# Shared experts' weight tiles issued from ScalarE's DMA queue instead of SyncE's

## The chip, the cores and the metric

One core of a Trainium2 chip runs the whole program. The metric is device time in microseconds of one execution. A core has five engines that run their own instruction streams and meet through semaphores: TensorE (PE), VectorE (DVE), ScalarE (ACT), GpSimd (POOL) and SyncE (SP). SP, ACT and POOL can each issue DMAs. The transfers themselves run on 16 DMA engines of the core.

## The reference

Two transformer blocks one after the other, on 256 tokens of width 1024, all in float32. The first has two layers; each has a mixer of three attention kinds, a cross attention to a memory, and a feed-forward part. The feed-forward part of layer 1 is the one that the change touches, a mixture of 8 experts of which each token takes 2:

```python
for e in range(N_EXPERTS):                      # 8
    out = out + gate[:, e:e + 1] * swiglu(t, w_gu[e], w_down[e])
# swiglu: (silu(t @ w_gate) * (t @ w_up)) @ w_down, with 1024 -> 2816 -> 1024
```

The weights of the eight experts are 8 x 35 MB (some 277 MB by the tensors' shapes), and all of them are read. The second block (an attention with a state-space part, then a pooling part) follows and is untouched.

## The kernel before

**Weights.** `weights` is a buffer of 5 slots of 128 x 4096 floats (2 MB each). SP fills a slot with one DMA and adds 16 to `slot{s}_landed`. PE adds 1 to `slot{s}_used` on its last matmul from the slot, and SP waits for that before it fills the slot again.

**The expert stage.** When no expert has more than 96 tokens (it is so here), the kernel gathers the tokens of each expert and works in 2 groups (`g`) of 4 experts. Experts 0, 1 and 2 of a group own one pass each (`q` = 0, 1, 2), in which they use 96 of the 128 rows of the array; the fourth, the shared expert, uses the last 32 rows in all three passes. So a step, called a row here, needs four tiles: one shared and three own. A group has 11 rows for up (`HID_CHUNKS`, each 256 hidden columns) and 6 for down (`FEW_DOWN`, the last one with half-size tiles of 1 MB); there are 34 rows in all, row 0 to row 33.

`few_slots` (L95) gives the slots: the shared tile of row r lies in slot r % 2, so there are two of them; the own tiles of each row lie in slots 2, 3 and 4, one buffer each. Own tile q of row r+1 can thus only be issued when pass q of row r has been done. `few_tiles` (L2064) lists the tiles in the order shared, own 0, own 1, own 2 for each row, and SP issues that list in order. The list's first five were issued before the stage.

PE (`few_group`, L715) does in each row pass 0, 1 and 2. Ahead of pass 0 it waits for the shared tile and own 0, ahead of pass 1 for own 1, ahead of pass 2 for own 2. It releases own 2 with the first matmul of the following row (`slot_owed`), and the shared slot with a matmul of the last quartet of pass 2. Behind pass 0 of an up row stand six transposes of the row before.

ACT has one silu for each pass of an up row (L1893), from the PSUM bank that the pass filled; DVE multiplies it with the other half (L1446). In the down rows ACT has nothing to do. Between the groups PE gathers the next group's tokens and sums the results of the first (`few_gather(1)`, `few_sum(0)`).

Of the kernel before, what the change touches and what calls it, by code (L numbers as in the profile page):

```python
# [69 lines left out]
NSLOT = 5  # L70
# [24 lines left out]
def few_slots(row):  # L95

    return row % 2, [2 + q for q in range(PASSES)]


def few_count(row, s):  # L100

    return row // 2 + 1 if s < 2 else row + 1
# [15 lines left out]
class Line:  # L118
# [15 lines left out]
    def next(self, name, k=1):  # L134

        self.seen[name] = self.seen.get(name, 0) + k
        return self.at(name, self.seen[name])
# [32 lines left out]
def program(nc, d, out, stop=None):  # L170
    ctx = ExitStack()
    with ctx:
# [5 lines left out]
        def sems(name):  # L178
            if name not in sem_table:
                sem_table[name] = ctx.enter_context(nc.semaphore(name))  # L180
            return sem_table[name]
# [102 lines left out]
        bank_mem = [ctx.enter_context(nc.psum_tensor(f"bank{i}", [P, 512], F32)) for i in range(4)]  # L284
        pairs = Banks("pair", 2, pair_mem)
        banks = Banks("bank", 4, bank_mem)
        jobs, tiles_used = {}, [0]
        ended_in = {}

        block = ctx.enter_context(nc.Block())  # L290
# [24 lines left out]
        def _(pe):  # L315
# [493 lines left out]
            def moe():  # L809
                pe.wait_ge(*L.next("chosen_ready"))  # L810

                upper, ones = const[:, C_UPPER:C_UPPER + P], const[:, C_ONES:C_ONES + P]
                o = begin(banks, ("places",))
                mm(o[:, 0:8], upper, chosen[:, 0, :], start=True, stop=True)
                mm(o[:, 8:16], ones, chosen[:, 0, :], start=True, stop=False)
                mm(o[:, 8:16], upper, chosen[:, 1, :], start=False, stop=True)
                mm(o[:, 16:24], ones, chosen[:, 0, :], start=True, stop=False)
                end(mm(o[:, 16:24], ones, chosen[:, 1, :], start=False, stop=True))
                pe.wait_ge(*L.next("count_ready"))
                largest = pe.value_load(most_i[0:1, 0:1], min_val=0, max_val=T)  # L820
                start = (counts(), list(pairs.uses), list(banks.uses), tiles_used[0], dict(L.seen))

                def begun():
                    return {k: v - start[0][k] for k, v in counts().items()}
                pairs.next = banks.next = 0
                rounds.update({s: sum(n % NSLOT == s for n in range(tiles_used[0])) for s in range(NSLOT)})
                with pe.If(largest < FEW + 1):
                    few_gather(0)
                    few_group(0)
                    few_gather(1)  # L830
                    few_sum(0)
                    few_group(1)
                    few_sum(1)
                    assert begun() == IN_FEW, begun()

                    for i in range(2):
                        for t in range(NT):
                            pe.wait_ge(*emptied(("few_sum", 1, i, t)))
                    pe.sem_inc(sems("banks_filled"), to_come("banks_filled", IN_FEW["banks_filled"]))
                    for s in range(2):  # L840
                        more = ALL_ROUNDS - few_count(FEW_ROWS - 2 + s, s)
                        pe.sem_inc(sems(f"slot{s}_landed"), 16 * more)
                        pe.sem_inc(sems(f"slot{s}_used"), more)
                few_seen = dict(L.seen)
                filled[0] = start[0]["banks_filled"]
                pairs.uses, banks.uses, tiles_used[0], L.seen = start[1], start[2], start[3], start[4]
                with pe.Else():

                    for s in range(NSLOT):
                        pe.wait_ge(*L.at(f"slot{s}_landed", 16 * (rounds[s] + 1)))  # L850
                        pe.sem_inc(sems(f"slot{s}_used"), 1)
                    tiles_used[0] += NSLOT
                    loop_experts(N_EXPERTS, PER_EXPERT, lambda: ffn_body(("ffn", 1)))
                    assert begun() == EACH, begun()

                    for i in range(2):
                        ring, b, _, _ = jobs[("ffn", 1), "down", i]
                        pe.wait_ge(*L.at(ring.emptied(b), ring.uses[b]))
                    pe.wait_ge(*L.at(f"slot{(tiles_used[0] - 1) % NSLOT}_used", tiles_used_at(0)))
                    for s in range(NSLOT):  # L860
                        pe.sem_inc(sems(f"slot{s}_landed"), 16 * (ALL_ROUNDS - EACH_ROUNDS))
                        pe.sem_inc(sems(f"slot{s}_used"), ALL_ROUNDS - EACH_ROUNDS)
                    if to_come("banks_filled", EACH["banks_filled"]):
                        pe.sem_inc(sems("banks_filled"), to_come("banks_filled", EACH["banks_filled"]))
                filled[0] = start[0]["banks_filled"] + max(EACH["banks_filled"], IN_FEW["banks_filled"])
                for ring in (pairs, banks):
                    for i in range(ring.n):
                        name = ring.emptied(i)
                        ring.uses[i] = start[0][name] + max(EACH[name], IN_FEW[name])
                assert tiles_used[0] == start[3] + NSLOT * EACH_ROUNDS  # L870
                tiles_used[0] = start[3] + NSLOT * ALL_ROUNDS
                L.seen = few_seen
# [913 lines left out]
                odd()  # L1786


        @block.scalar
        def _(act):  # L1790
            L = Line(act, sems)
# [69 lines left out]
            for l in range(DEPTH):  # L1861
# [17 lines left out]
                if on(f"ffn{l}"):  # L1879
                    if l == 0:  # L1880
                        ffn_body(("ffn", l))
                    else:
                        act.wait_ge(*L.next("top_gap"))
                        act.activation(rstd[:, :, 1], rstd[:, :, 0], ACT.Exp).then_inc(sems("second_exp"), 1)
                        act.wait_ge(*L.next("count_ready"))
                        largest = act.value_load(most_i[0:1, 0:1], min_val=0, max_val=T)
                        with act.If(largest < FEW + 1):
                            for g in range(N_GROUPS):
                                for c in range(HID_CHUNKS):
                                    for q in range(PASSES):  # L1890
                                        act.wait_ge(*filled(("few_up", g, c, q)))
                                        o, _ = bank(("few_up", g, c, q))
                                        act.activation(few_silu[:, (PASSES * c + q) % 4, :], o[:, 0:256], ACT.Silu)\  # L1893
                                           .then_inc(sems("few_silu_done"), 1)
                        with act.Else():
                            with L.loop(N_EXPERTS, PER_EXPERT):
                                ffn_body(("ffn", l))
                    root()
# [137 lines left out]
        def _(sp):  # L2036
# [3 lines left out]
            def load(src, width):  # L2040

                i = n[0]
                n[0] += 1
                into(i % NSLOT, i // NSLOT, src, width)

            def into(s, before, src, width):
                if before:
                    sp.wait_ge(*L.at(f"slot{s}_used", before))
                sp.dma_start(weights[:, s, 0:width], src).then_inc(sems(f"slot{s}_landed"), 16)

            def stream(src, k_tiles, widths, group):
                for c, k0, nk, w, off in weight_tiles(k_tiles, widths, group):
# [7 lines left out]
                    load(down[:, k0 * 1024:(k0 + nk) * 1024], nk * 1024)  # L2060
                    k0 += nk


            def few_tiles(first):  # L2064

                rounds = [sum(i % NSLOT == s for i in range(first)) for s in range(NSLOT)]
                row = 0
                for g in range(N_GROUPS):
                    mine = [GROUP * g + SHARED] + [GROUP * g + q for q in range(PASSES)]
                    parts = [("moe_up", c * 4096, 4096) for c in range(HID_CHUNKS)]  # L2070
                    parts += [("moe_down", 1024 * sum(FEW_DOWN[:i]), 1024 * nk) for i, nk in enumerate(FEW_DOWN)]
                    for name, at, width in parts:
                        shared, owns = few_slots(row)
                        for e, s in zip(mine, [shared] + owns):
                            yield s, rounds[s] + few_count(row, s) - 1, d[name][e][:, at:at + width], width
                        row += 1

            sp.dma_start(h[:, :, :], d["x"].rearrange("(t p) n -> p t n", p=P)).then_inc(sems("x_landed"), 16)
            sp.dma_start(norm_par[:, 0, :, :].rearrange("p a n -> p (a n)"), d["norms"][0:1, :].to_broadcast([P, 2 * D]))\
# [3 lines left out]
            for l in range(DEPTH):  # L2083
# [14 lines left out]
                if on(f"ffn{l}"):  # L2098
                    if l == 0:
                        expert(d["ffn_up"][0], d["ffn_down"][0])  # L2100
                    else:
                        first = n[0]
                        order = list(few_tiles(first))
                        for tile in order[:NSLOT]:
                            into(*tile)
                        sp.wait_ge(*L.next("count_ready"))
                        largest = sp.value_load(most_i[0:1, 0:1], min_val=0, max_val=T)
                        with sp.If(largest < FEW + 1):
                            for tile in order[NSLOT:]:
                                into(*tile)  # L2110
                        n[0] = first + NSLOT
                        with sp.Else():
                            before = n[0]
# [172 lines left out]
```

## Time and profile before

| | |
|---|---|
| Median of 3 runs | 2481.23 us (2477.7 to 2481.24) |
| Profiled execution | 2480.64 us, of which the span 2478.8 us |
| PE busy | 2300.5 us, 93% of the span |
| DVE, ACT, POOL busy | 26%, 9%, 2% |
| Queue of SP's DMAs | 466.03 MB, 47.2% of the 16 engines' span |
| Expert stage | some 715 us of the span, from 1153 to 1868 us |

Busy time is the time in which an engine has an instruction running; several matmuls that run side by side in parts of the array count once. The span is from the first to the last instruction, and the execution's own time is 1.8 us longer. A DMA line gives the time from the issue to the landing of the last of its 16 parts. L numbers are lines of the kernel; L324 is the helper through which all matmuls go, L2049 the line that issues all weight tiles.

### The profile page before, as it was taken

Reading aid. Unit: us, or ns where it says so; the run is one execution under the profiler, and the core shown is the slowest. Engines: PE = TensorE matmul, PEld = TensorE weight load, DVE = VectorE, ACT = ScalarE, POOL = GpSimd, SP = SyncE. Lnnn points to the kernel's source line nnn. Section 1 sums busy time; section 2 is a strip of 40 time slices with the busy share of each in tenths; the row PEclk is TensorE's granted clock in tenths of the full one; section 3 lists DMA queues with packets and bytes.
Section 4 is the critical chain, followed back from the end, with each engine's and each line's share of the span. In section 5 each row is a group of like instructions: output and inputs, shape, how many; then the busy total and the mean of one; then the engine's idle time right before and its main releaser. Section 6 shows DMA issues by size and latency. Waiting matters only on the chain.

```text
span 2478.8 us, 25691 instructions
## 1 busy us (share of the span) xinstructions
PE 2300.5 (93%) x11554; PEld 1128.5 (46%) x11554; DVE 636.6 (26%) x1124; ACT 233.7 (9%) x493; POOL 54.7 (2%) x58
## 2 busy tenths in 40 slices
PE   7998999899899979988999999999997998787998
PEld 3444445787344434443333333333333455443683
DVE  2433312200114242233001002001004066963011
ACT  0122001000001310010000000000000024210000
POOL 0000000000000000000000000000000000320000
PEclk9999999999999999998999999999998999678999
DMA  7304432433522044133999987999986411014340
GB/s 319 134 18 153 170 140 98 170 127 111 214 111 95 26 179 169 68 159 153 388 390 392 402 358 312 387 391 390 403 358 259 157 68 52 0 44 194 119 153 17
DMA packets 38816, 486.13 MB, mean 196 GB/s; under 512 B 4352, under 2 KB 4384, under 8 KB 7472
## 3 DMA queue, kind: packets, MB, share of 16 engines
q1 hardware_dynamic: 35264, 466.03, 47.2%
q0 software_dynamic: 3440, 18.42, 2.0%
q8 instruction: 94, 1.54, 0.2%
q14 instruction: 18, 0.15, 0.0%
HBM read 483.38 MB, written 1.05 MB: 195 GB/s over the span
## 4 chain that ended last, share of the span: by engine, by line
PE 88%; DVE 10%; issue 1%; ACT 0%; DMA 0%; POOL 0%; DVEq 0%; ACTq 0%; PEldq 0%; POOLq 0%
PE pair L324 55%; PE bank L324 33%; DVE big L1620 2%; DVE att L1103 1%; DVE big L1715 1%; DVE stats L1120 1%; DVE h L1162 1%; DVE big L1728 0%; DVE hT L1103 0%; DVE big L1103 0%; DVE h L1158 0%; DVE prob L1240 0%; DVE big L1704 0%; DMA h<-in_x 0%; DVE att L1179 0%
## 5 line engine op out<-in xcount | busy, mean ns | idle before, releaser
L324 PE MATMUL pair<-weights,hT 128*128 128x512 f32 (+1 forms) x1384 | 613.8, 600 | 7.4 <-DVE hT L1103 7.4
L324 PE MATMUL bank<-weights,att 128*32 128x512 f32 x4224 | 457.8, 593 | 0.0
L324 PEld LDWEIGHTS pair<-weights,hT 128*128 128x128 f32 x1384 | 261.6, 193 | 326.9 <-issue 314.3
L324 PE MATMUL pair<-weights,big 128*32 128x512 f32 (+1 forms) x1968 | 396.0, 592 | 3.4 <-ACT big L1840 1.7
L324 PEld LDWEIGHTS bank<-weights,att 128*32 128x32 f32 x4224 | 135.0, 110 | 306.5 <-issue 306.3
L324 PEld LDWEIGHTS pair<-weights,big 128*32 128x32 f32 (+1 forms) x1968 | 153.6, 133 | 235.6 <-issue 231.0
L324 PE MATMUL pair<-hT,weights 128*128 128x256 f32 x960 | 207.6, 379 | 0.8 <-DVE hT L1103 0.8
L324 PEld LDWEIGHTS pair<-hT,weights 128*128 128x128 f32 x960 | 182.3, 190 | 26.2 <-DVE hT L1103 1.0
L1103 DVE COPY big<-pair 128x1024 f32<-128x1024 f32 (+2 forms) x53 | 58.5, 1104 | 356.8 <-PE pair L324 356.8
L1446 DVE TENSOR_TENSOR big<-head_gain,bank 128x256 f32<-128x256 f32 x66 | 27.8, 421 | 422.5 <-ACT head_gain L1893 422.5
L324 PE MATMUL pair<-weights,att 128*128 128x512 f32 x256 | 115.9, 608 | 10.5 <-DVE att L1339 6.0
L1103 DVE COPY att<-bank 64x512 f32<-64x512 f32 (+4 forms) x120 | 69.8, 603 | 206.9 <-PE bank L324 206.5
L324 PE MATMUL bank<-att 64*128 64x256 f32 (+3 forms) x288 | 84.0, 427 | 16.9 <-DVE att L1103 10.3
L1893 ACT ACTIVATE head_gain<-bank 128x256 f32<-128x256 f32 x66 | 25.4, 384 | 600.8 <-PE bank L324 600.8
L324 PEld LDWEIGHTS pair<-weights,att 128*128 128x128 f32 x256 | 49.0, 193 | 70.4 <-issue 67.6
L324 PE MATMUL bank<-weights,big 128*32 128x512 f32 x704 | 77.8, 592 | 0.0
L324 PEld LDWEIGHTS bank<-att 128*128 128x128 f32 (+2 forms) x288 | 52.4, 194 | 46.9 <-issue 18.8
L324 PE MATMUL bank<-const,big 128*128 128x128 f32 (+2 forms) x328 | 46.3, 294 | 12.2 <-DVE big L1211 9.3
L1827 ACT ACTIVATE prob<-bank,smax 128x256 f32<-128x256 f32 x64 | 29.8, 470 | 264.4 <-DVE smax L1230 264.4
L324 PE MATMUL bank<-const,h 128*128 128x128 f32 x96 | 18.2, 370 | 38.9 <-DVE h L1162 38.9
L324 PE MATMUL bank<-probT,big 128*64 128x256 f32 (+1 forms) x192 | 48.9, 387 | 3.2 <-ACT probT L1798 3.2
L324 PEld LDWEIGHTS bank<-const,big 128*128 128x128 f32 (+2 forms) x328 | 38.6, 135 | 26.7 <-DVE big L1211 11.7
(221 smaller groups left out, 1288.4 us busy)
## 6 DMA issues: line engine op xcount, KB each, us to landing
weights<-in_moe_up SPq DMA_DIRECT2D x88, 2048.0 KB, 11.0
weights<-in_moe_down SPq DMA_DIRECT2D x40, 2048.0 KB, 11.6
weights<-in_w_in SPq DMA_DIRECT2D x18, 2048.0 KB, 7.4
weights<-in_ffn_up SPq DMA_DIRECT2D x11, 2048.0 KB, 7.2
weights<-in_even_in SPq DMA_DIRECT2D x10, 2048.0 KB, 7.8
weights<-in_mem_wkv SPq DMA_DIRECT2D x8, 2048.0 KB, 7.3
weights<-in_odd_in SPq DMA_DIRECT2D x8, 2048.0 KB, 7.2
norm_par<-in_norms POOLq DMA_DIRECT2D x10, 1024.0 KB, 7.3
```

What stands on the lines that cost most here:

```text
L324: ins = pe.matmul(o, lhsT, rhs, **flags)
L1103: ve.tensor_copy(dst, src(o)).then_inc(free, 1)
L1120: ins = ve.bn_stats(stats[:, t, c, :], src[:, t, 512 * c:512 * c + 512])
L1162: ins = ve.scalar_tensor_tensor(h[:, t, :], h[:, t, :], rstd[:, t, 0:1], b, ALU.mult, ALU.add)
L1446: ve.tensor_tensor(few_hid[:, c % 2, q, :], few_silu[:, (PASSES * c + q) % 4, :], o[:, 256:512], ALU.mult).then_inc(free, 1)
L1620: link(ve.tensor_tensor(o, a, b, op))
L1715: ins = ve.tensor_tensor_scan(scanned[:, c, i, :], rho[:, j:j + 1].to_broadcast([P, T]), w[:, i, :], 0.0, ALU.mult, ALU.add)
L1827: ins = act.activation(p, src, ACT.Exp, bias=smax[:, i % 2, t:t + 1], scale=1.0 if masked else scale, accum_out=ssum[:, i % 2, t:t + 1])
L1893: act.activation(few_silu[:, (PASSES * c + q) % 4, :], o[:, 0:256], ACT.Silu)\
```

## The change

In the expert stage the shared tiles from row 2 on (32 tiles, slots 0 and 1) leave SP's list, and ACT issues them. In the up rows ACT does so ahead of the first silu of a row: in row r it issues the shared tile of row r+1. Behind the up rows of group 0 it issues six, behind those of group 1 five. Each keeps its wait for `slot{s}_used` and its landing semaphore. SP keeps the own tiles in their order. `into` and `few_tiles` move up so that both engines can use them. All other loads stay.

```diff
+        def into(eng, L, s, before, src, width):
+            if before:
+                eng.wait_ge(*L.at(f"slot{s}_used", before))
+            eng.dma_start(weights[:, s, 0:width], src).then_inc(sems(f"slot{s}_landed"), 16)
...
                         with act.If(largest < FEW + 1):
+                            shared = [tile for tile in list(few_tiles(moe_first[0]))[NSLOT:] if tile[0] < 2]
+                            ahead = iter(shared)
                             for g in range(N_GROUPS):
                                 for c in range(HID_CHUNKS):
                                     for q in range(PASSES):
+                                        if q == 0 and (g, c) != (0, 0):
+                                            into(act, L, *next(ahead))
                                         act.wait_ge(*filled(("few_up", g, c, q)))
                                         o, _ = bank(("few_up", g, c, q))
                                         act.activation(few_silu[:, (PASSES * c + q) % 4, :], o[:, 0:256], ACT.Silu)\
                                            .then_inc(sems("few_silu_done"), 1)
+                                for _ in FEW_DOWN:
+                                    tile = next(ahead, None)
+                                    if tile is not None:
+                                        into(act, L, *tile)
...
                         with sp.If(largest < FEW + 1):
                             for tile in order[NSLOT:]:
-                                into(*tile)
+                                if tile[0] >= 2:
+                                    into(sp, L, *tile)
```

## Rows read from the trace of the kernel before

**Rows 1.** The page: span, and the chain that ended last, by engine.

```profile
span 2478.8 us, 25691 instructions
...
PE 88%; DVE 10%; issue 1%; ACT 0%; DMA 0%; POOL 0%; DVEq 0%; ACTq 0%; PEldq 0%; POOLq 0%
```

**Rows 2.** Windows: the whole expert stage, and one of its up rows.

```profile
core 0: us, PE busy (x) PEld busy (x) DVE busy (x) ACT busy (x) POOL busy (x), PEclk, DMA share, GB/s
1153.00:1868.00 715.00, 714.94 (x6466) 229.67 (x6462) 62.34 (x110) 26.65 (x67) 0.00 (x0) 1.00 0.92 377
1303.80:1325.34 21.54, 21.54 (x200) 6.77 (x199) 2.13 (x5) 1.16 (x3) 0.00 (x0) 1.00 0.96 395
```

**Rows 3.** Timeline (start, duration): an up row's end; SP issues own 2.

```profile
1296.31 0.38 ACT L1893 ACTIVATE head_gain<-bank 128x256 f32<-128x256 f32 x1 [6.50 <-PE bank L324]
...
1297.06 0.33 SPq L2049 DMA_DIRECT2D weights<-in_moe_up  x1
```

**Rows 4.** SP's issues behind it: own 2; then shared, own 0, own 1.

```profile
weights<-in_moe_up SPq DMA_DIRECT2D x1, 2048.0 KB, 9.2
...
L2049 SPq DMA_DIRECT2D weights<-in_moe_up x3: 327/328/431, 1297.4 to 1310.9; - x3
...
DMA to landing us min/median/max: 10.3/12.9/13.7
```

**Rows 5.** Timeline: weight load that opens pass 2, and SP's next issue.

```profile
1353.34 0.13 PEld L324 LDWEIGHTS bank<-weights,att 128*32 128x32 f32 x4 [0.30 <-issue]
...
1354.00 0.33 SPq L2049 DMA_DIRECT2D weights<-in_moe_up  x1
```

**Rows 6.** DMA views: a tile alone; one beside q0's; packets from 1113 to 1118 us.

```profile
weights<-in_moe_up SPq DMA_DIRECT2D x1, 2048.0 KB, 7.2
...
weights<-in_moe_up SPq DMA_DIRECT2D x1, 2048.0 KB, 11.5
...
q1 hardware_dynamic: 85, 1.39, 65.1%
q0 software_dynamic: 92, 0.75, 35.5%
```

**Rows 7.** L2049, shared to own 1: first row, worst up, worst down, last.

```profile
L2049 SPq DMA_DIRECT2D weights<-in_moe_up x3: 328/328/431, 1168.2 to 1181.7; - x3
...
DMA to landing us min/median/max: 9.7/12.5/13.2
...
weights<-in_moe_up SPq DMA_DIRECT2D x1, 2048.0 KB, 14.2
...
L2049 SPq DMA_DIRECT2D weights<-in_moe_down x3: 328/328/972, 1797.9 to 1810.2; - x3
...
DMA to landing us min/median/max: 11.8/13.6/14.1
...
L2049 SPq DMA_DIRECT2D weights<-in_moe_down x3: 327/327/432, 1839.1 to 1851.7; - x3
...
DMA to landing us min/median/max: 6.5/8.9/12.2
```

**Rows 8.** Row 16: own 2 and the shared tile issued; landings; pass 2 opens.

```profile
1487.17 0.33 SPq L2049 DMA_DIRECT2D weights<-in_moe_down  x1
...
1487.55 0.43 SPq L2049 DMA_DIRECT2D weights<-in_moe_up  x1
...
weights<-in_moe_down SPq DMA_DIRECT2D x1, 1024.0 KB, 4.9
...
weights<-in_moe_up SPq DMA_DIRECT2D x1, 2048.0 KB, 10.5
...
1492.56 0.13 PEld L324 LDWEIGHTS bank<-weights,big 128*32 128x32 f32 x4 [0.30 <-issue]
```

**Rows 9.** Windows: a PE pause of 3.43 us, and the stretch behind it.

```profile
201.93:205.36 3.43, 0.00 (x1) 0.00 (x0) 3.20 (x13) 0.55 (x1) 0.00 (x0) 1.00 0.91 306
205.80:209.20 3.40, 3.27 (x16) 2.41 (x14) 2.57 (x4) 0.00 (x0) 0.00 (x0) 0.50 0.77 251
```

More of the change, by code:

```diff
@@ L286, in program @@
         banks = Banks("bank", 4, bank_mem)
-        jobs, tiles_used = {}, [0]
+        jobs, tiles_used, moe_first = {}, [0], [0]
         ended_in = {}
@@ L825, in moe @@
                 pairs.next = banks.next = 0
+                moe_first[0] = tiles_used[0]
                 rounds.update({s: sum(n % NSLOT == s for n in range(tiles_used[0])) for s in range(NSLOT)})
@@ L1786, in _, with few_tiles @@
                 odd()
+        def into(eng, L, s, before, src, width):
+            if before:
+                eng.wait_ge(*L.at(f"slot{s}_used", before))
+            eng.dma_start(weights[:, s, 0:width], src).then_inc(sems(f"slot{s}_landed"), 16)
+        def few_tiles(first):
+            rounds = [sum(i % NSLOT == s for i in range(first)) for s in range(NSLOT)]
+            row = 0
+            for g in range(N_GROUPS):
+                mine = [GROUP * g + SHARED] + [GROUP * g + q for q in range(PASSES)]
+                parts = [("moe_up", c * 4096, 4096) for c in range(HID_CHUNKS)]
+                parts += [("moe_down", 1024 * sum(FEW_DOWN[:i]), 1024 * nk) for i, nk in enumerate(FEW_DOWN)]
+                for name, at, width in parts:
+                    shared, owns = few_slots(row)
+                    for e, s in zip(mine, [shared] + owns):
+                        yield s, rounds[s] + few_count(row, s) - 1, d[name][e][:, at:at + width], width
+                    row += 1
         @block.scalar
@@ L2043, in load @@
                 n[0] += 1
[L2044 to L2049, printed above, removed]
+                into(sp, L, i % NSLOT, i // NSLOT, src, width)
             def stream(src, k_tiles, widths, group):
@@ L2061, in expert @@
                     k0 += nk
[L2064 to L2076, printed above, removed]
             sp.dma_start(h[:, :, :], d["x"].rearrange("(t p) n -> p t n", p=P)).then_inc(sems("x_landed"), 16)
@@ L2109, in _ @@
                             for tile in order[NSLOT:]:
-                                into(*tile)
+                                if tile[0] >= 2:
+                                    into(sp, L, *tile)
                         n[0] = first + NSLOT
```

## The prediction

> **What bounds the kernel now.** Read first the page's chain of waits, for which engine sets the end: PE holds 88% of it and DMA none [rows 1]. Then the stretch that the change touches, by windows: in the 715.00 us of the expert stage PE is busy 714.94 us, in one up row 21.54 of 21.54 us, at granted clock 1.00, so 2.4 GHz [rows 2]. There is no pause in which PE waits for a tile. The DMA engines are close behind: 0.92 of the stage, 0.96 of that row. So PE sets the time, and each tile lands a few us ahead of the pass that needs it. The question is which tile has how much to spare, and in what order they come. That is read from the DMA landings, one issue at a time.
>
> Take the row whose pass 2 ends at about 1296.3 us, where ACT's silu starts [rows 3]. SP issues own 2 of the next row (call it row r) at 1297.06 and the shared tile of row r+1 right behind it at 1297.43. Own 2 lands after 9.2 us, the shared tile after 13.7, own 0 after 12.9, own 1 after 10.3 [rows 4]. Own 2 is needed when pass 2 of row r opens. The weight load that opens a pass 2 stands at 1353.34, and SP's issue of own 1, which the end of pass 1 releases, at 1354.00 [rows 5]: the deadline is some 0.65 us before own 1's issue. Here that is 1310.9 - 0.65 = 1310.3, and own 2 landed at 1306.3: 4.0 us to spare. The shared tile landed at 1311.2 and has until row r+1 opens, near 1318. So today's order on SP's queue is the right one: the urgent tile first, the patient one behind it.
>
> **The change part by part.**
>
> *SP loses 32 issues.* One is 0.33 us of a queue that otherwise waits for PE [rows 3]. Own 2 still waits for the same release, and own 0, own 1 for theirs. Nothing is earlier: 0.
>
> *ACT gains 32 waits and issues.* In an up row the wait is for the end of the row before, which has passed when ACT gets there, since the silu of that row's pass 2 stands ahead of it. The next silu is 6.5 us away [rows 3], so an issue of about 0.33 us (SP's; the trace has none on ACT) is hidden. Queued behind the waiting instruction are silus alone, and DVE's product and the bank behind them; if the cover were gone, each issue would cost PE at most its own 0.33 us. In the down rows ACT has no other work. In the gathering between the groups it has none either. 0, with bounds 0 and 32 x 0.33 = 10.6 us, and I take 0.
>
> *The shared tile is issued a little earlier.* In an up row ACT can issue when its silu is over, 1296.31 + 0.38 = 1296.69, against 1297.06 for own 2: a lead of 0.37 us. In a down row there is no silu, and the lead is 1297.06 - 1296.31 = 0.75 us. PE doesn't wait for this tile, so the lead alone is worth nothing.
>
> *Own 2 and the shared tile now lie on two queues.* This is the term that counts. The nearest rows are those where POOL's queue q0 works beside SP's q1, from 1113 to 1118 us: 92 packets of the one and 85 of the other, that is packet by packet in turn, though q0's were half as large (0.75 MB to 1.39) [rows 6]. A tile issued there landed after 11.5 us, against 7.2 alone [rows 6]. In turn, two tiles of 2 MB that start together both end when both are done. So own 2 would land where the shared tile lands now, less the lead. Were the shared tile served wholly first, own 2 would end there as well; only a preference for own 2 would spare it.
>
> The Trainium skill says the same of queues in general: its page "DMA: Bandwidth & Descriptors", section "Queues, rings and completion order", has each DMA engine take turns between its queues packet by packet, and the section "Issuing engines are not separate DMA queues" says that issuing from several engines saves only the sequencers' time. It speaks against the change: by it there is no more bandwidth to be had, and the urgent tile has to share. The trace agrees as far as it has two queues at once [rows 6].
>
> *The price by rows.* Own 2's lateness in a row is (issue of the shared tile + its landing time) - (issue of own 1 - 0.65) - lead. In the example: 1297.43 + 13.7 - 1310.3 = 0.9, less 0.37 = 0.5 us. I worked it out for the 30 rows of full tiles between the first pair and the last [rows 7]; 20 are up, 10 down. The first: 1168.2 + 13.2 - 1181.0 = 0.4, less 0.37: nothing. The worst up row: landing 14.2, 1.4 late, less 0.37 = 1.0. The worst down row: 1797.95 + 14.1 - 1809.5 = 2.5, less 0.75 = 1.8 (down rows lack the transposes, so their deadline comes 0.9 us sooner). The last: 1839.1 + 12.2 - 1851.05 = 0.25, less 0.75: nothing. Over the up rows 8 of 20 are late and add up to 2.7 us; of the down rows 6 of 10, with 4.9 us. A stall doesn't breed the next: own 0 and own 1 of the following row are issued before it, on the same queue and with the same bytes ahead of them.
>
> *Row 16* is a case by itself. Its tiles are of 1 MB, its passes half as long, and beside its own 2 goes a full shared tile for row 17. Own 2 is issued at 1487.17, lands after 4.9 us at 1492.1, and pass 2 opens at 1492.56: 0.5 us to spare. The shared tile lands at 1487.55 + 10.5 = 1498.05 [rows 8]. In turn own 2 comes at 1498.05 - 0.75 = 1497.3: 4.7 us of stall. PE has nothing else there, and all behind it (the rest of row 16, the gathering) moves along. After a pause of 3.43 us at clock 1.00 the next 3.40 us ran at 0.50, 1.2 GHz [rows 9]. Such a stretch costs half of itself: 3.4 / 2 = 1.7 us more.
>
> Row 33 has the small tiles too, but no shared tile is behind its own 2: 0.
>
> *Sum.* 2.7 + 4.9 + 4.7 + 1.7 = 14.0 us. Ahead of each weight load PE's loader idles 0.30 us [rows 5], so a tile may be 0.3 us later without moving a matmul: with that, 1.3 + 3.2 + 4.4 + 1.7 = 10.6. What it costs PE to take up again after a wait no row shows; I let the two stand against each other and take the middle, 12.3. Against the profiled execution's 2480.64 us that gives 2493 us; this execution is 0.6 us below the median of the runs shown, so it serves for both. Bounds: with no lead at all the terms are 6.8 + 10.4 + 5.5 + 1.7 = 24.4 us (2505); with own 2 always in time, 0 (2481).
>
> **The rivals.**
>
> *Own 2 is in time after all: 2481.* The mechanism is a preference: two hardware queues might be served in the order in which a tile's work reached them, or ACT's start later by more than the 4.0 us that own 2 has to spare above, so that own 2 is through first. It decides in row 16: own 2 has 0.5 us to spare there, and everything hinges on whether it is ahead of the shared tile. For it: q0 beside q1 is a software queue, not a second hardware one, and the late landings hang on the slowest of the 16 parts, which may be slower in the profiled execution than in others. Against it: the turns of [rows 6]. If only the spread of the parts shrank, row 16 would stay and the time be 2481 + 6 = 2487. Chance of no change from this: 0.22.
>
> *Faster.* The shared tile's lead fills some of the DMA engines' pause at each row's start, and SP's queue is free sooner. It could only pay where PE waits for a tile, and the stage holds 0.06 us of such time [rows 2]: 2480.6 at best. Chance 0.04.
>
> *Much slower.* The packets of two hardware queues hinder each other. A row moves 8 MB in 21.54 us, with the DMA engines busy 0.96 of it [rows 2]. If the two tiles that share (9.2 of 13.7 us) took 10% more, own 2 would be 1 us later in all 32 rows, and 2493 + 28 = 2521. Against it: the 1113 to 1118 us stretch moved 2.14 MB in 5 us, 428 GB/s, no less than one queue's best. Chance 0.06, of which half beyond my range.
>
> **How the numbers follow.** The forecast, own 2 late by sharing in turn, has 0.68. Its time is 2493 and its own range 2486 to 2505. Some 5 us, 0.2%, is what a measurement here can tell from no change. Slower by more than that: forecast and the heavy case, 0.74, less 0.02 for a forecast that comes out small: 0.72. Same: 0.24. Faster: 0.04. The range takes in the case of no change at its lower end and the bound without a lead at its upper one: 2480 to 2506.
>
> **What the profile of the changed kernel would show.** Right: PE busy below the stage's length for the first time, by some 10 us, with a pause of 4 to 5 us at row 16, ahead of the matmuls of its pass 2, and a granted clock of 0.50 behind it. Own 2's landing goes from 7 to 10 us to 11 to 14 in each row, the shared tile's from 12 to 14 by little. ACT's issues start 0.4 us (up) or 0.75 us (down) before SP's. A second hardware queue with some 65 MB. The period of most up rows stays 21.54 us, that of the late ones grows by under 1.5. Wrong: own 2 landing in 7 to 10 us as now, own 0 or own 1 later than 13 us (then the model of the order is wrong), silus delayed by ACT's issues, or pauses in rows that I have as in time.

## The result: 15 us slower, and the profile after

The changed kernel takes 2494.86 us (median of 5 runs, 2491.78 to 2501.76) against 2479.5 us before. The ratio is 1.0064, 95% interval 1.0048 to 1.0081. Measured again on another chip (e5 below) it came to 2495.73 against 2479.02 us, 1.0062 (1.0049 to 1.0075). The forecast was 2493 us, with 0.72 on slower by more than 0.2%.

The page of the kernel after: queues (q1 is SyncE's, q10 ScalarE's; packets, MB, share of 16 engines' span), and the chain that ended last. Against [rows 1], DMA now has a share of the chain.

```profile
span 2493.0 us, 25691 instructions
...
q1 hardware_dynamic: 30656, 401.02, 40.5%
q10 hardware_dynamic: 4608, 65.01, 6.9%
...
PE 82%; DVE 10%; DMA 6%; issue 1%; ACT 0%; POOL 0%; DVEq 0%; ACTq 0%; PEldq 0%; POOLq 0%
...
PE pair L324 52%; PE bank L324 30%; DMA weights<-in_moe_up 4%; DMA weights<-in_moe_down 3%; DVE big L1621 2%; DVE att L1104 1%; DVE big L1716 1%; DVE stats L1121 1%; DVE h L1163 0%; DVE big L1729 0%; DVE hT L1104 0%; DVE big L1104 0%; DVE h L1159 0%; DVE prob L1241 0%; DVE big L1705 0%
```

Windows of the kernel after: the expert stage, now some 732 us long. PE was busy all of it in [rows 2]; now 11.7 us are missing. (The window is 17 us longer: the stage itself by 15.7, and it starts 0.9 later.)

```profile
core 0: us, PE busy (x) PEld busy (x) DVE busy (x) ACT busy (x) POOL busy (x), PEclk, DMA share, GB/s
1153.00:1885.00 732.00, 720.33 (x6478) 225.57 (x6470) 62.30 (x110) 26.58 (x67) 0.00 (x0) 1.00 0.91 368
```

Waits of the kernel after in the stage (us in total, times, longest). No line of this kind stood there before. The loader's waits (PEld) and the matmuls' (PE) are the same pauses seen twice.

```profile
PEld bank L324 <- DMA weights<-in_moe_up: 13.2, 9, 2.7
PEld bank L324 <- DMA weights<-in_moe_down: 12.4, 7, 3.9
PE bank L324 <- DMA weights<-in_moe_down: 6.5, 4, 3.0
PE bank L324 <- DMA weights<-in_moe_up: 5.0, 5, 1.8
```

All of these waits come in pass 2. The timeline of the kernel after at the end of row 1, against [rows 3]: ACT issues the shared tile (L1793 is the common `into`) 0.75 us ahead of SP's own 2, and then the landings of the two.

```profile
1189.54 0.38 ACT L1917 ACTIVATE head_gain<-bank 128x256 f32<-128x256 f32 x1 [6.50 <-PE bank L324]
1189.55 0.34 ACTq L1793 DMA_DIRECT2D weights<-in_moe_up  x1
...
1190.30 0.33 SPq L1793 DMA_DIRECT2D weights<-in_moe_up  x1
...
weights<-in_moe_up ACTq DMA_DIRECT2D x1, 2048.0 KB, 15.2
...
weights<-in_moe_up SPq DMA_DIRECT2D x1, 2048.0 KB, 15.1
```

The worst of the up rows was in [rows 7] a shared tile with 14.2 us, and nobody waited for it. Here own 2 itself needs 15.1.

**The rule that ties a row's length to a landing.** In the 20 up rows of full tiles, the time from one own 2's issue to the next is 21.54 us and what own 2's landing exceeds 13.55 us. Worked out from the issues and landings of the kernel after:

| Row | own 2 lands after | row lasts | 21.54 + (landing - 13.55) |
|---|---|---|---|
| 2 | 15.07 | 23.06 | 23.06 |
| 9 | 14.88 | 22.87 | 22.87 |
| 22 | 14.23 | 22.23 | 22.22 |
| 24 | 13.69 | 21.68 | 21.68 |
| 26 | 12.89 | 21.54 | (in time) |
| 27 | 15.57 | 23.56 | 23.56 |

The 13.55 is fitted to these rows; with it the rule holds in all 20 within 0.01 us, and with the same number in the second trace of this kernel and in e1, e2, e8 and e9. So in the up rows the whole loss is own 2's lateness; nothing else lengthens a row.

**Row 16.** Timeline of the kernel after at the start of its pass 2, then windows: the pause and what follows. [Rows 8] had the matmuls run through here.

```profile
1503.99 0.20 PEld L324 LDWEIGHTS bank<-weights,big 128*32 128x32 f32 x8 [3.89 <-DMA weights<-in_moe_down]
1503.99 1.94 PE L324 MATMUL bank<-weights,big 128*32 128x512 f32 x8 [2.98 <-DMA weights<-in_moe_down]
...
1501.01:1503.99 2.98, 0.00 (x0) 0.00 (x0) 1.22 (x1) 0.00 (x0) 0.00 (x0) 0.90 1.04 443
1503.99:1507.50 3.51, 3.51 (x20) 0.91 (x24) 0.14 (x1) 0.00 (x0) 0.00 (x0) 0.60 1.00 429
```

Own 2 of row 16 landed after 8.9 us instead of 4.9, PE paused 2.98 us, and the clock was at 0.60 on average in the 3.5 us behind, as after the pause of [rows 9]. (The clock of 0.90 in the pause itself says that some 0.6 us of the half-clock stretch lay in it, where it cost nothing; the rest cost 1.4 us.) From own 2 of row 16 to own 2 of row 17 it takes 14.85 us in place of 10.30, 4.5 more.

The stage's account, by differences of these row lengths against before:

| | up rows | down rows | row 16 | sum |
|---|---|---|---|---|
| predicted, strict deadline | 2.7 | 4.9 | 6.4 | 14.0 |
| predicted, deadline 0.3 later | 1.3 | 3.2 | 6.1 | 10.6 |
| changed kernel | 6.9 | 4.2 | 4.5 | 15.7 |
| the same, second trace | 4.6 | 5.6 | 4.8 | 14.9 |

The two profiled executions before and after are 14.2 us apart (2480.64, 2494.86); the program outside the stage came out 1.5 us shorter in the second. Traces of kernels that do not lose (e3, e4 below) have sums of 0.4 to 0.6, so a difference of some tenths says nothing.

### The profile page after: what moved, and what is told of

Its sections match the earlier page's. It is cut to its first block, busy times and chain, and to the rows that moved or that the text cites. A ratio compares the mean times of both kernels' runs of the same rounds, so it can differ in the third digit from the quotient of the medians.

```text
span 2493.0 us, 25691 instructions
## 1 busy us (share of the span) xinstructions
PE 2303.2 (92%) x11554; PEld 1124.1 (45%) x11554; DVE 636.0 (26%) x1124; ACT 233.6 (9%) x493; POOL 54.6 (2%) x58
## 3 DMA queue, kind: packets, MB, share of 16 engines
q10 hardware_dynamic: 4608, 65.01, 6.9%
## 4 chain that ended last, share of the span: by engine, by line
PE 82%; DVE 10%; DMA 6%; issue 1%; ACT 0%; POOL 0%; DVEq 0%; ACTq 0%; PEldq 0%; POOLq 0%
PE pair L324 52%; PE bank L324 30%; DMA weights<-in_moe_up 4%; DMA weights<-in_moe_down 3%; DVE big L1621 2%; DVE att L1104 1%; DVE big L1716 1%; DVE stats L1121 1%; DVE h L1163 0%; DVE big L1729 0%; DVE hT L1104 0%; DVE big L1104 0%; DVE h L1159 0%; DVE prob L1241 0%; DVE big L1705 0%
## 5 line engine op out<-in xcount | busy, mean ns | idle before, releaser
L324 PE MATMUL bank<-att 64*128 64x256 f32 (+3 forms) x288 | 85.9, 434 | 16.7 <-DVE att L1104 10.1
L324 PEld LDWEIGHTS bank<-weights,big 128*32 128x32 f32 x704 | 22.5, 111 | 62.1 <-issue 49.6
## 6 DMA issues: line engine op xcount, KB each, us to landing
weights<-in_moe_up SPq DMA_DIRECT2D x68, 2048.0 KB, 11.7
weights<-in_moe_down SPq DMA_DIRECT2D x30, 2048.0 KB, 11.6
```

The lines of the kernel that those rows point to most:

```text
L324: ins = pe.matmul(o, lhsT, rhs, **flags)
```

## Experiments

All times are against runs of the kernel before on the same chip. "Stage" is the sum of row differences in one trace, as in the table above (for e7 and e10 with 0.8 us of row 17).

| Run | what | median, before | ratio (95%) | stage |
|---|---|---|---|---|
| e1 | one queue, shared tile ahead of own 2 | 2487.18, 2479.98 | 1.0031 (1.0020 to 1.0042) | +9.1 |
| e2 | change, but row 17's tile on SP | 2486.9, 2479.98 | 1.0035 (1.0021 to 1.0049) | +5.2 |
| e3 | before, small DMAs on ACT | 2479.28, 2479.98 | 1.0000 (0.9991 to 1.0009) | +0.6 |
| e4 | change, half the shared tile | 2480.32, 2479.98 | 1.0001 (0.9992 to 1.0010) | +0.4 |
| e5 | the change again | 2495.73, 2479.02 | 1.0062 (1.0049 to 1.0075) | +14.9 |
| e6 | only row 17's tile on ACT | 2484.18, 2479.02 | 1.0024 (1.0015 to 1.0032) | +5.1 |
| e7 | shared tile held until own 2 lands | 2521.44, 2479.02 | 1.0157 (1.0125 to 1.0188) | +46 |
| e8 | e1 without row 16 | 2485.94, 2479.02 | 1.0033 (1.0020 to 1.0046) | +4.3 |
| e9 | change without the head start | 2489.37, 2481.27 | 1.0035 (1.0021 to 1.0048) | +9.5 |
| e10 | shared tile held until pass 0 ends | 2485.7, 2481.27 | 1.0022 (1.0012 to 1.0031) | +7.4 |
| e11 | e1 without the head start | 2490.12, 2479.51 | 1.0050 (1.0037 to 1.0064) | +8.0 |
| e12 | change, own 2 given the head start | 2480.83, 2479.51 | 1.0007 (0.9998 to 1.0016) | +1.6 |

Theory 1 is the forecast's: what costs is own 2 coming behind the shared tile's bytes. The first rival is that ScalarE's issues, or a second queue as such, cost.

**e1, the order alone.**

```diff
+rest = order[NSLOT:]
+for i in range(len(rest) - 1):
+    if rest[i][0] == 4 and rest[i + 1][0] < 2:        # own 2, then the next row's shared tile
+        rest[i], rest[i + 1] = rest[i + 1], rest[i]
```

> All weight tiles stay on SyncE's queue; in each row the shared tile of the next row is issued ahead of own 2 instead of behind it. Theory 1 (the loss comes from own 2 landing behind the shared tile's bytes, whatever queue they are on): own 2 lands 11 to 14 us after its issue, row 16 loses about 4.5 us and the late rows some 3 to 10 us more, so 8 to 15 us slower than before. Rival 2 (it is the second hardware queue, or ScalarE's issues, that cost time): within 2 us of before, for there is neither here. Rival 3 (both: the order costs, and two queues spread the landings further): slower than before by 6 to 10 us, and by less than the changed kernel.

7.2 us slower, with no second queue and nothing new on ACT. So the order by itself costs, in this run about half of the change's loss (e11 below, another one-queue version, lost 10.6). Its waits in the stage:

```profile
PEld bank L324 <- DMA weights<-in_moe_down: 11.6, 7, 3.9
PE bank L324 <- DMA weights<-in_moe_down: 5.8, 5, 3.0
PEld bank L324 <- DMA weights<-in_moe_up: 3.3, 4, 1.1
```

Row 16's pause of 3.0 us is as in the changed kernel and the down rows are near it (3.6 us, against 4.2 and 5.6); the up rows are not (0.6 us in all, against 6.9 and 4.6). That is the outcome of the third theory.

**e2 and e6, row 16.** e2 gives row 17's shared tile back to SP, e6 leaves only that one on ACT (ACT's side of the edit is not printed here).

```diff
 # e2, SP; e6 has != 16
-    if tile[0] >= 2:
+    n_shared += tile[0] < 2
+    if tile[0] >= 2 or n_shared == 16:
         into(sp, L, *tile)
```

> The changed kernel, with one of the 32 shared tiles (that of row 17, beside the half-size own 2 of row 16) back on SyncE's queue behind own 2. Theory 1: the pause of 2.98 us and the 3.4 us at half clock at row 16 go, 4.5 us faster than the changed kernel, so some 10 us slower than before. Rival 2 (ScalarE's issues or the second queue as such): one issue in 32, 0.5 us faster than the changed kernel.

> The kernel before with one of the 32 shared tiles, that of row 17, on ScalarE's queue. Both theories: own 2 of row 16 lands some 4 us later, a pause of 3 us and 3.4 us of half clock, 4.5 us slower than before; no pause anywhere else.

e6 cost 5.2 us in its median and 5.0 us at row 16 in its trace, with no other row longer by more than 0.2: one tile of 32 makes a third of the loss. The windows of e6 show it; PE is busy 335.00 of 335.00 us ahead of row 16.

```profile
1153.00:1488.00 335.00, 335.00 (x3098) 104.21 (x3094) 23.83 (x46) 12.66 (x33) 0.00 (x0) 1.00 0.93 380
1490.00:1510.00 20.00, 16.60 (x98) 6.57 (x91) 6.34 (x9) 0.00 (x0) 0.00 (x0) 0.91 1.00 427
```

e2 kept 6.9 us of the loss, where some 10 were expected; in its trace row 16 lasts as before, which is the 4.5 us, but the late rows make 5.2 where the change's two traces had 11.1 and 10.1. Why they cost less there is not shown. The two together, 1.0035 and 1.0024, come near the change's 1.0062.

**e3, ScalarE's share.** The 32 waits and issues on ACT, with 2 KB in place of the tile.

```diff
 for q in range(PASSES):
+    if q == 0 and (g, c) != (0, 0):
+        small(next(ahead))      # waits for the shared slot, DMA of 128 x 16 bytes to a spare buffer
     act.wait_ge(*filled(("few_up", g, c, q)))
```

> The kernel before, with every tile on SyncE's queue, and ScalarE in addition doing the 32 waits of the change at its places and issuing behind each a DMA of 128 x 16 bytes (2 KB, into a spare buffer) instead of the tile. Theory 1: ScalarE's waits and issues are hidden, within 2 us of before. Rival 2a (the waits and issues on ScalarE delay silus, products and banks): 5 to 15 us slower, as the changed kernel.

The same as before. ScalarE's waits and issues are hidden, and the rival that blamed them falls.

**e4, fewer bytes on the second queue.** ScalarE loads the first half of each shared tile.

```diff
-into(act, L, *tile)
+into(act, L, s, before, src[:, 0:width // 2], width // 2)
```

> The changed kernel, but ScalarE loads only the first half of each shared tile (the rest of the slot keeps old data, so part of the shared experts' sums is left out). Theory 1: the two tiles that share have 3 MB instead of 4, own 2 lands some 2.4 us sooner (9 to 12 us after its issue), under the deadline of 13.5 us in nearly all rows; row 16 still has 2 MB in place of 3 to wait for, its pause falls from 3 us to under 1; in all 0 to 3 us slower than before. Rival 2 (the second queue or ScalarE's issues as such): the number of issues is the same, 10 to 15 us slower than before.

The same as before, with as many issues on as many queues. In the up rows own 2 landed after 9.6 us on average (10.6 at most); only row 16 had a wait left:

```profile
PEld bank L324 <- DMA weights<-in_moe_down: 1.4, 1, 1.4
PE bank L324 <- DMA weights<-in_moe_down: 0.5, 1, 0.5
```

A second queue as such, with 32 half tiles on it, costs nothing. The bytes that own 2 has to share with do.

**e5, the change again; e8, e1 without row 16.**

> The changed kernel as it is, on the same chip as the next three. Swapping the order on one queue cost 7.2 us, the change as first measured 15. Theory 1 (order alone): the excess is chance or the chip, and it comes out 7 to 11 us slower than before. Theory 3 (two queues add a spread of landings to the cost of the order): 13 to 17 us slower again.

> One queue, order swapped as before, but not for row 16 (own 2 of row 16 ahead of the shared tile of row 17). Theory 1: the 4.9 us at row 16 go, 2 to 4 us slower than before is left from the late rows.

e5 shows that the change's excess over e1 is no chance; against e11 the intervals leave it open. e8 is a miss by its time: 6.9 us slower, hardly less than e1's 7.2, where 2 to 4 were expected. In its trace row 16 lasts 10.30 us again and the late rows add 4.3, as expected; its five runs lie between 2482.93 and 2489.49 and the profiled one is the lowest. So what the late rows cost differs by some us from run to run, and e8 doesn't resolve row 16; e6 does, with 11 runs.

**e7 and e10, the shared tile held back.** Both were meant to give own 2 the engines for itself.

```diff
 # e7, behind the silu of pass 0; e10 waits for "slot2_used" (the end of pass 0)
+act.wait_ge(*L.at("slot4_landed", 16 * own_2[0]))
 into(act, L, s, before, src, width)
```

> The changed kernel, but ScalarE waits for the landing of own 2 before it issues the shared tile, and does so behind the first silu of the row. 32 tiles are on the second queue as in the change. Theory 1: own 2 lands 7 to 10 us after its issue again, no pause at row 16, and the shared tile now shares with own 0 and own 1, which have time; 0 to 3 us slower than before. Rival 2 (a second queue as such costs): 8 us or more slower than before.

> The changed kernel, but ScalarE issues each shared tile only when pass 0 of the row is over (it waits for slot 2's release, as SyncE does for own 0), so level with own 0, 6 us behind own 2. Holding it back to own 2's landing made the kernel 39 us slower, for the shared tile was issued 8 to 9 us later than before and had only 7 us to spare. Theory 1 with that: own 2 lands after 7 to 10 us as before, no pause at row 16; shared tile and own 0 land 12 to 14 us after their issue, 18 to 20 into the row, where 20.9 is the deadline: 0 to 6 us slower than before. Rival 2 (a second queue as such costs): 10 us or more.

e7 failed by far, and it isn't the queue: own 2 landed after 7.2 to 9.7 us, and row 16 had no pause. Another tile became the late one. Timeline of e7 in one row, with the landing of its shared tile:

```profile
1221.99 0.33 ACTq L1793 DMA_DIRECT2D weights<-in_moe_up  x1
...
weights<-in_moe_up ACTq DMA_DIRECT2D x1, 2048.0 KB, 14.5
...
1236.50 3.49 PE L324 MATMUL bank<-weights,att 128*32 128x512 f32 x20 [2.96 <-DMA weights<-in_moe_up]
```

1221.99 + 14.5 = 1236.5: PE stands until the shared tile is there. It was issued 9.1 us behind own 2, where before it was 0.4, and had 7 us to spare; the expectation counted own 2's time and not this tile's. e10, which holds it back to 6.1 us behind own 2 (e7: 7.2 to 9.8), lost 4.4 us, inside what was expected, with waits at the rows' starts. So the shared tile has a deadline too, and of the orders tried here the one before meets both, and e12's all but once.

**e9, e11 and e12, the head start.** In e9 ScalarE also waits for the release of own 2, so that both tiles are issued in the same 0.01 us. e11 does so in e1. e12 adds two silus on a spare buffer, so that own 2 is 0.90 us ahead.

```diff
+act.wait_ge(*L.at("slot4_used", own_2[0]))
+for _ in range(2):                                  # e12 only
+    act.activation(spare[:, 256:512], spare[:, 0:256], ACT.Silu).then_inc(sems("paused"), 1)
+    act.wait_ge(*L.next("paused"))
 into(act, L, s, before, src, width)
```

> The changed kernel, but ScalarE waits in addition for the release that SyncE waits for before own 2, so that the shared tile is issued level with own 2 and not 0.75 us ahead. Own 2's end is set by the bytes of both, so it should come later by the lead. In two traces of the changed kernel a row is longer than 21.54 us by exactly what own 2's landing exceeds 13.55 us; with 0.75 us more on each landing that rule gives 14 more. Theory 1: 22 to 30 us slower than before. Rival 4 (own 2 is late only because the shared tile's packets are ahead of it when it comes, so that level is better): at most 10 us slower.

> One queue, order swapped, but SyncE waits for own 2's release ahead of the shared tile, so the two are issued 0.4 us apart at the time of today's own 2, and the head start of 0.8 us is gone. Without the head start two queues lost 8 us instead of 15: the last of the 16 parts then came 1.4 us behind the first, not 2.2. Theory 5 (a head start while own 1's last parts still land spreads the landings, whatever the queue): the spread falls from 1.8 to some 1.4 here too, own 2 lands 12 to 13.5 us after its issue; 5 to 8 us slower than before, most of it at row 16. Rival (the spread belongs to two queues): it stays at 1.8, 7 to 12 us slower.

> The changed kernel, but ScalarE waits for own 2's release and then runs two silus on a spare buffer, each waited for, before it issues the shared tile: own 2 is now some 0.8 us ahead of it, on the other queue. Theory 6 (what is first in line gets its first packets alone, then they take turns): own 2 is through after 8 to 10 us, the shared tile lands when both are done, as before; no pause at row 16; 0 to 3 us slower than before, with all 32 tiles on the second queue. Rival (in turn from the start, own 2 ends last but one packet): own 2 lands after 11 us or more, row 16 pauses 2 us or more, 4 us or more slower.

e9 refuted my account of the lead. It lost 8.1 us, not 22 to 30, which is the range of its rival 4 (level is better), though own 2 was still late there. Its first parts did come later (11.5 us after the issue on average, 10.9 in the change), as the account had it; but the last of the 16 came 1.4 us behind the first and not 2.2, so the landings rose no higher than 13.65 in the up rows, which cost 0.2 us. Down rows and row 16 lost as in the change (4.3 and 5.1). e11 had 1.5 us of spread and up rows at 0.9 in its trace (the fastest of its five runs), but its runs are 10.6 us slower, above the 5 to 8 of theory 5 and inside the rival's 7 to 12; e1 and e11 can't be told apart by their intervals. So theory 5 isn't shown. With two queues the spread was smaller when both tiles were issued level (1.4 in one trace, against 2.2 to 2.4), but e12, where own 2 has the head start and not the shared tile, has 2.2 as well; with one queue nothing is shown.

e12 is the decisive one. All 32 tiles are on the second queue, 65.01 MB, and the loss is gone. Timeline of e12 at a row's end, the two landings behind it, then its one wait in the stage:

```profile
1296.38 0.33 SPq L1794 DMA_DIRECT2D weights<-in_moe_up  x1
1296.39 0.87 ACT L1918 ACTIVATE spare<-spare 128x256 f32<-128x256 f32 x2 [0.38 <-PE bank L325]
1297.28 0.33 ACTq L1794 DMA_DIRECT2D weights<-in_moe_up  x1
...
weights<-in_moe_up SPq DMA_DIRECT2D x1, 2048.0 KB, 10.9
...
weights<-in_moe_up ACTq DMA_DIRECT2D x1, 2048.0 KB, 14.9
...
PEld bank L325 <- DMA weights<-in_moe_down: 2.6, 1, 2.6
```

Own 2 landed after 10.7 us on average in the up rows (12.8 at most), all in time, and row 16 took 10.30 us. That is later than the 8 to 10 us expected, since its last part came 2.2 us behind its first (8.4), but the pause and the loss are theory 6's. Which of the two tiles is issued first, by 0.75 or by 0.90 us, decides some 14 to 15 us; issued level, they cost 8. No run points to a version that beats the kernel before: there PE waits 0.06 us in the whole stage [rows 2].

## Why the prediction was right, point by point

- *What bounds the kernel, and that no gain was to be had.* Right. PE without a pause left nothing to win; the rival "faster" had no ground.
- *Own 2 lands when both tiles are through.* Right. The sum had the shared tile's landing less the lead, for the example 14.1 - 0.4 us after own 2's issue. Own 2 landed after 13.1 and 13.2 us on average in the up rows of the two traces (before: 7.95), and no up row lengthened for another reason (the rule above). e1, e4 and e12 show it by order, bytes and head start. That the two take turns, from which it was argued, held only in part: the shared tile was first served alone (last section). The prediction had said that own 2 would then end at the same time, so nothing in the sum hung on it; but the same behaviour is why e12 loses nothing.
- *ACT's waits and issues cost nothing.* Right (e3).
- *Row 16.* Right in place and mechanism: one pause of 3 us and a stretch at half clock. The size was 6.4 us where 4.5 to 5.0 came: own 2 landed at 8.9 us and not 10.1, since its last part came 0.6 us behind its first, where I had taken over the shared tile's 1.7; and of the 3.4 us at half clock 0.6 fell into the pause.
- *The down rows.* 4.9 predicted, 4.2 and 5.6 measured.
- *The up rows.* The term that was mis-sized: 2.7 us (1.3 with the later deadline), against 6.9 and 4.6. Two errors worked against each other and a third decided. The deadline is 13.55 us after own 2's issue, 0.35 later than the strict one (13.20, from 1354.00 - 0.65 and an issue of own 2 at 1340.15), so the 0.30 us of the loader's idle time were indeed to be had. The lead in an up row is 0.75 us, not 0.37: ACT issues at the start of the silu, 1189.55 to 1189.54 above, and doesn't wait for its end. Both make the loss smaller: put into the prediction's own working they leave 0.3 us of the 2.7. But the 16 parts of own 2 land further apart, 2.2 to 2.4 us from first to last on average, where the shared tile's had 1.75 before, and some rows reach 15 us.
- *The sum.* 12.3 us was taken as the middle of 10.6 and 14.0; the stage lost 15.7 and 14.9, the medians 15.4 and 16.7. That it came so near is in part luck: in the up rows a lead and a deadline that were sized too low stood in for part of a spread that had not been foreseen, and row 16 was put 1.6 to 1.9 us too high. What it costs PE to take up again after a wait, left open there, is within 0.01 us of nothing by the rule.
- *The rival "own 2 in time"* was possible: e12 is this case, made by 1.65 us of difference in ScalarE's issue. *Much slower* through hindering packets was not seen. The queues' lines over the stage, before and then after:

```profile
q1 hardware_dynamic: 18986, 268.35, 91.3%
...
q1 hardware_dynamic: 14385, 203.43, 67.1%
q10 hardware_dynamic: 4608, 65.01, 23.3%
```

The same 268 MB took 91.3% of 715 us before and 90.4% of 732 us after, 653 and 662 us: 1.4% more, where this rival had 10% for the tiles that share.

Why own 2's 16 parts land further apart with two queues, unless both tiles are issued level, is open. The traces have 1.4 us on average in e9, 2.2, 2.4 and 2.2 in the change twice and e2, 2.2 in e12, 1.8 and 2.0 in the one-queue e1 and e8, 1.3 before; from row to row it varies by about 1 us, so only the ends of this series are apart. In row 2, whose issues are shown above, 14 parts of own 2 landed by 11.6 us, the last two at 13.7 and 15.1.

## What to carry to other kernels

A queue that issues in order of urgency is worth something that the issue time doesn't show: put on a second queue, the patient transfer took half of the DMA engines here, and more when it was first. Ask of each transfer its own deadline and add the bytes that may now go ahead of it; if a move to another queue is wanted, see that the urgent tile is issued first; here 0.9 us was enough. Look for the odd row, with small tiles and short passes: one of 32 transfers made a third of this loss.

## What was not expected of the hardware

Packets of the kernel after in two windows of 3 us: from 1190.9, when both tiles have been issued, and from 1194.5.

```profile
q10 hardware_dynamic: 58, 0.95, 81.7%
q1 hardware_dynamic: 3, 0.02, 1.3%
...
q10 hardware_dynamic: 40, 0.66, 55.0%
q1 hardware_dynamic: 32, 0.52, 41.9%
```

The queues do take turns, but not from the start: with 0.75 us of head start, ScalarE's queue had the engines for itself until 1194, 3.7 us after own 2's issue, some 3 to 5 packets of 16 KB on each of the 16 engines. Only then did the two alternate. e12 shows the mirror image, and e9 the case without a head start. Packets of e12 from 1297.3 to 1300.9 us, when both tiles of the row shown above have been issued, and from 1301.5 to 1304.5; then of e9 from 1297.0 to 1301.0, both tiles issued at 1297.19:

```profile
q1 hardware_dynamic: 81, 1.29, 99.9%
...
q1 hardware_dynamic: 44, 0.72, 56.0%
q10 hardware_dynamic: 33, 0.54, 42.0%
...
q1 hardware_dynamic: 37, 0.56, 46.7%
q10 hardware_dynamic: 32, 0.52, 31.4%
```

In e12 own 2 is served alone until 3.7 us after the shared tile's issue, and by then some 80 of its 128 packets of 16 KB have started; that is how 0.90 us of head start keep it in time. In e9 the two alternate from their first packets. What holds the second tile back for 3.7 us, at the engines or ahead of them, no run shows.

The Trainium skill's page "DMA: Bandwidth & Descriptors", section "Queues, rings and completion order", has the engines take turns packet by packet; by that, the second window of the kernel after agrees, and its first one, with 58 packets to 3, is not what the rule alone leads one to expect.
